# Splitting the next slot ahead of the norm, unread products between two tiles' transposes, and a first panel begun by parts

## The reference

```python
x = x + hybrid_mixer(rmsnorm(x, ...))              # gated delta rule and mLSTM
x = x + memory_cross_attention(rmsnorm(x, ...), rmsnorm(mem, ...), ...)
x = x + peer_ffn(rmsnorm(x, ...), ...)             # 128 key pairs, top 16, experts
x = rmsnorm(x, norm_final_w)
# second block: each sub-layer is followed by a layer norm
x = post_norm(x, swiglu(x, ...), g, b)             # layer_norm(DN_ALPHA * x + sub, g, b)
x = post_norm(x, chunked_sgu_mixer(x, ...), g, b)
x = post_norm(x, swiglu(x, ...), g, b)
# keys and values (selected, window, compressed) are made of this x
x = post_norm(x, swiglu(x, ...), g, b)
x = post_norm(x, sparse_attention(x, ...), g, b)
x = post_norm(x, swiglu(x, ...), g, b)
```

## Time and profile before

| | us or share |
|---|---|
| median of three runs | 2404.67 (2404.33 to 2405.97) |
| span of the profiled execution | 2405.3; no other time of that execution is given |
| TensorE busy | 2268.6, 94% |
| VectorE busy | 1544.9, 64% |
| ScalarE busy | 1126.1, 47% |
| mean granted TensorE clock | 0.964 |
| HBM over the span | 161 GB/s |

### The profile page before, as it was taken

The page is one execution under the profiler, slowest core; times in us unless marked ns, Lnnn a source line. Parts: engine busy times, 40 slices in busy tenths (PEclk is TensorE's granted clock), DMA queues, the critical chain, the costliest instruction groups (busy, mean ns, idle before and its releaser), DMA issues. The chain is left out here.

```text
span 2405.3 us, 38363 instructions
## 1 busy us (share of the span) xinstructions
PE 2268.6 (94%) x15466; PEld 2086.1 (87%) x15466; DVE 1544.9 (64%) x2713; ACT 1126.1 (47%) x1961; POOL 51.6 (2%) x26
## 2 busy tenths in 40 slices
PE   8979888999999999999999999999999999988998
PEld 8867676999999997888878998979998899867997
DVE  7866445999888985666655456665456545575554
ACT  5523334455554445555555344444443434474443
POOL 0121000100000000000000000000000000000000
PEclk9989889999999999999999999999999999889999
DMA  6362233355444445666646555535555655303552
GB/s 260 139 67 91 88 129 127 120 178 182 158 142 148 144 147 177 193 195 194 195 127 251 182 187 211 193 134 215 191 178 192 228 183 186 125 19 123 197 188 105
DMA packets 78310, 390.25 MB, mean 162 GB/s; under 512 B 9772, under 2 KB 12716, under 8 KB 49741
## 3 DMA queue, kind: packets, MB, share of 16 engines
q1 hardware_dynamic: 76684, 383.59, 46.3%
q0 software_dynamic: 1040, 4.19, 1.6%
q10 hardware_dynamic: 432, 0.33, 0.0%
HBM read 382.83 MB, written 5.24 MB: 161 GB/s over the span
## 5 line engine op out<-in xcount | busy, mean ns | idle before, releaser
L246 DVE TENSOR_TENSOR split_slots<-ring,split_slots 128x1024 fp32r<-128x1024 f32 x406 | 481.9, 1232 | 333.7 <-ACT split_slots L237 333.6
L339 PE MATMUL banks<-x_transposed_hi,split_slots 128*128 128x256 f32 x1920 | 549.8, 286 | 8.8 <-DVE split_slots L246 5.2
L340 PE MATMUL banks<-x_transposed_lo,split_slots 128*128 128x256 f32 x1920 | 547.9, 285 | 0.0
L341 PE MATMUL banks<-x_transposed_hi,split_slots 128*128 128x256 f32 x1920 | 547.6, 285 | 0.0
L237 ACT ACTIVATE split_slots<-ring 128x1024 fp32r<-128x1024 f32 x406 | 404.4, 1049 | 222.6 <-PE banks L341 197.2
L350 DVE SCALAR_TENSOR_TENSOR expert_lo<-ring,expert_hi 128x512 fp32r<-128x512 f32 x512 | 363.2, 714 | 173.8 <-ACT expert_hi L345 172.7
L345 ACT ACTIVATE expert_hi<-ring 128x512 fp32r<-128x512 f32 x512 | 323.2, 632 | 266.8 <-PE banks L341 266.7
L339 PEld LDWEIGHTS banks<-x_transposed_hi,split_slots 128*128 128x128 f32 x1920 | 372.2, 194 | 11.5 <-DVE split_slots L246 5.6
L340 PEld LDWEIGHTS banks<-x_transposed_lo,split_slots 128*128 128x128 f32 x1920 | 372.1, 194 | 1.5
L341 PEld LDWEIGHTS banks<-x_transposed_hi,split_slots 128*128 128x128 f32 x1920 | 372.1, 194 | 0.0
L339 PE MATMUL banks<-x_transposed_hi,expert_hi 128*128 128x256 f32 x1024 | 296.8, 290 | 5.5 <-DVE expert_lo L350 5.5
(11 more groups left out here) (463 smaller groups left out, 3431.8 us busy)
## 6 DMA issues: line engine op xcount, KB each, us to landing
ring<-in_ffn_w SPq DMA_DIRECT2D x132, 1024.0 KB, 4.8
ring<-in_peer_u SPq DMA_DIRECT2D x128, 512.0 KB, 3.5
ring<-in_peer_v SPq DMA_DIRECT2D x128, 512.0 KB, 4.3
ring<-in_w_in SPq DMA_DIRECT2D x16, 1024.0 KB, 5.1
ring<-in_sgu_w_in SPq DMA_DIRECT2D x16, 1024.0 KB, 4.8
ring<-in_peer_wq SPq DMA_DIRECT2D x8, 1024.0 KB, 5.0
ring<-in_sgu_w_out SPq DMA_DIRECT2D x8, 1024.0 KB, 4.8
ring<-in_kv_w SPq DMA_DIRECT2D x6, 1024.0 KB, 4.8
```

The lines of the kernel that those rows point to most:

```text
L246: ins = dve.tensor_tensor(self.parts[:, b, 1, p], self.k.w.slot(g)[:, p], self.parts[:, b, 0, p].bitcast(F32), ALU.subtract)
L339: pe.matmul(out, lh, rh, start=start, stop=False)
L340: pe.matmul(out, lh, rl, start=False, stop=False)
L341: return pe.matmul(out, ll, rh, start=False, stop=stop)
```

## The change

Three things, in the diff's order. Split buffers are numbered by the slot's number in the whole program instead of in its stage, so the next stage's first slot goes to the buffer of slot `slots - 3`; in PostNorm the begun slot's split always stands ahead of the norm, after a wait for that slot, and in RmsNorm it moves from last place to ahead of the norm (ScalarE) and ahead of the first add (VectorE). TensorE gets plain 128x128 float32 products of two constant tiles into bank 1, which nothing reads (`stand_in`): 3 after tile 0's transposes and, except in PostNorm 0, 7 when tile 1 is centred and 4 when its root is there; in RmsNorm 4, 6 and 4. Tile 1's transposes move out of the norm and into `high_first` of the next stage where there is one in the same block: with x on the right (weights stationary) the first four transposes, the 16 products of chunks 0 to 3, the other four transposes, the 16 products of chunks 4 to 7; with x on the left (`spatial_gating`) the 16 products of tile 0, then all eight transposes, then tile 1's products by halves. That first panel goes to bank 0 instead of 4. Where a barrier follows, `last` (or no `begin`) keeps the eight transposes in the norm.

```diff
@@ class Splitter
+    def buffer(self, n):
+        return (self.g0 + n) % self.buffers
...
-        g, b = self.g0 + n, n % self.buffers
+        g, b = self.g0 + n, self.buffer(n)
...
@@ class Beginning
+        self.b = self.g % BUFFERS
...
-        act.activation(k.split_parts[:, 0, 0, p], k.w.slot(self.g)[:, p], ACT.Copy).then_inc(self.high_done, 1)
+        act.activation(k.split_parts[:, self.b, 0, p], k.w.slot(self.g)[:, p], ACT.Copy).then_inc(self.high_done, 1)
...
@@ def high_first
-    before.rows_high(pe)
-    for j in range(2):
-        for c in range(DC):
+    started = []
+    def banks():
+        for signal, value in before.banks_read:
+            pe.wait_ge(signal, value)
+    def high(j, chunks):
+        for c in chunks:
             (lh, ll), (rh, rl) = operands(j, c)
-            pe.matmul(out(j), lh, rh, start=(j == 0 and c == 0), stop=False)
+            pe.matmul(out(j), lh, rh, start=not started, stop=False)
+            started.append(c)
             if x_on_right:
                 pe.matmul(out(j), ll, rh, start=False, stop=False)
             else:
                 pe.matmul(out(j), lh, rl, start=False, stop=False)
+    near, far = range(DC // 2), range(DC // 2, DC)
+    if before.turn is None:
+        banks()
+        if before.highed:
+            pe.wait_ge(*before.highed)
+        for j in range(2):
+            high(j, range(DC))
+    else:
+        if not x_on_right:
+            pe.wait_ge(before.highed[0], 2)
+            high(0, range(DC))
+        before.turn(pe, near)
+        if x_on_right:
+            banks()
+        else:
+            before.turn(pe, far)
+        pe.wait_ge(before.highed[0], 3)
+        for j in range(2) if x_on_right else (1,):
+            high(j, near)
+        if x_on_right:
+            before.turn(pe, far)
+        pe.wait_ge(before.highed[0], 4)
+        for j in range(2) if x_on_right else (1,):
+            high(j, far)
     before.rows_low(pe)
...
@@ def turn_chunks
-def turn_chunks(pe, k, src, tile, ready, first=0, normed=None):
-    for c in range(DC):
+def turn_chunks(pe, k, src, tile, ready, first=0, normed=None, own=range(8)):
+    for c in own:
         if normed is not None and c % 4 == 0:
             pe.wait_ge(normed, 2 * tile + c // 4 + 1)
         ins = pe.transpose(k.psum[:, first + 2 * tile + c // 4, c % 4 * P:(c % 4 + 1) * P], src[:, c * P:(c + 1) * P],
                            k.ident[:, :])
         if c % 4 == 3:
             ins.then_inc(ready, 1)
+def stand_in(pe, k, n):
+    for _ in range(n):
+        pe.matmul(k.psum[:, 1, 0:P], k.ident[:, :], k.ones[:, :], start=True, stop=True)
...
@@ class PostNorm
-        self.free = (slots - 1) // BUFFERS * BUFFERS
-        self.early = self.free < slots - 2
+        self.free = slots - BUFFERS
...
-        if self.begin and self.early:
+        if self.begin:
             self.begin.lows(dve)
...
-            if not self.early:
-                self.begin.lows(dve)
             for b in range(4):
                 self.low(dve, b)
...
-        if self.begin and self.early:
+        if self.begin:
             self.split.finished(act, self.free)
             self.begin.highs(act)
...
-            if not self.early:
-                act.wait_ge(self.tile_done, TILES)
-                self.begin.highs(act)
             self.high(act, 2)
             self.high(act, 3)
...
-        self.k.before = Before((self.tile_done, TILES), (self.highed, 4), (self.written, 4), ((self.written, 1),))
+        self.k.before = Before((self.tile_done, TILES), (self.highed, 4), (self.written, 4), ((self.written, 1),),
+                               turn=self.turn_last)
         self.k.gains_free = self.normed
+    def turn_last(self, pe, chunks):
+        turn_chunks(pe, self.k, self.k.x[:, 1, :], 1, self.banks, 4, self.normed, chunks)
     def tensor(self, pe):
         if self.begin:
-            for i in range(TILES):
-                turn_chunks(pe, self.k, self.k.x[:, i, :], i, self.banks, 4, self.normed)
+            turn_chunks(pe, self.k, self.k.x[:, 0, :], 0, self.banks, 4, self.normed)
+            stand_in(pe, self.k, 3)
+            if self.which != 0:
+                pe.wait_ge(self.negated, 2)
+                stand_in(pe, self.k, 7)
+                pe.wait_ge(self.rooted, 2)
+                stand_in(pe, self.k, 4)
+            if self.last:
+                self.turn_last(pe, range(DC))
...
@@ class RmsNorm
+        self.free = slots - BUFFERS
...
+        if self.begin:
+            self.begin.lows(dve)
         add(0)
         dve.wait_ge(*self.gain_landed)
...
-        if self.begin:
-            self.begin.lows(dve)
...
+        if self.begin:
+            self.split.finished(act, self.free)
+            self.begin.highs(act)
         act.activation(self.warm[:, :], k.eps[:, 0:1], ACT.Sqrt)
         squares(0)
...
-        if self.begin:
-            act.wait_ge(self.tile_done, TILES)
-            self.begin.highs(act)
+    def turn_last(self, pe, chunks):
+        turn_chunks(pe, self.k, self.xn[:, 1, :], 1, self.banks, 4, self.normed, chunks)
     def tensor(self, pe):
-        for i in range(TILES):
-            turn_chunks(pe, self.k, self.xn[:, i, :], i, self.banks, 4, self.normed)
+        turn_chunks(pe, self.k, self.xn[:, 0, :], 0, self.banks, 4, self.normed)
+        stand_in(pe, self.k, 4)
+        pe.wait_ge(self.added, 2)
+        stand_in(pe, self.k, 6)
+        pe.wait_ge(self.rooted, 2)
+        stand_in(pe, self.k, 4)
+        if not self.begin:
+            self.turn_last(pe, range(DC))
...
@@ def swiglu, def spatial_gating
-        norm = PostNorm(k, ctx, split, gains, which, 3 * UNITS, final)
+        norm = PostNorm(k, ctx, split, gains, which, 3 * UNITS, final, last=compress is not None)
-        norm = PostNorm(k, ctx, split, gains, 1, slots, squares=v[:, :, 0:D])
+        norm = PostNorm(k, ctx, split, gains, 1, slots, squares=v[:, :, 0:D], last=True)
-                    return k.psum[:, 4 + m % 2, j * SEQ:(j + 1) * SEQ]
+                    return k.psum[:, 4 + m % 2 if m else 0, j * SEQ:(j + 1) * SEQ]
-                act.activation(dst, bank2(k, 4 + m % 2), ACT.Gelu).then_inc(panel_read, 1)
+                act.activation(dst, bank2(k, 4 + m % 2 if m else 0), ACT.Gelu).then_inc(panel_read, 1)
```

More of the change, by code:

```diff
@@ L255, in panel @@
     def panel(self, n):
-        return [self.parts[:, n % self.buffers, q, :].rearrange("p (c n) -> p c n", c=DC) for q in range(2)]
+        return [self.parts[:, self.buffer(n), q, :].rearrange("p (c n) -> p c n", c=DC) for q in range(2)]
     def rows(self, n):
-        return [self.parts[:, n % self.buffers, q, :].rearrange("p (r n) -> p r n", r=2) for q in range(2)]
+        return [self.parts[:, self.buffer(n), q, :].rearrange("p (r n) -> p r n", r=2) for q in range(2)]
     def finished(self, engine, n, i=0, per=0):
@@ L289, in low @@
         dve.wait_ge(self.high_done, half + 1)
-        ins = dve.tensor_tensor(k.split_parts[:, 0, 1, p], k.w.slot(self.g)[:, p], k.split_parts[:, 0, 0, p].bitcast(F32),
-                                ALU.subtract)
+        ins = dve.tensor_tensor(k.split_parts[:, self.b, 1, p], k.w.slot(self.g)[:, p],
+                                k.split_parts[:, self.b, 0, p].bitcast(F32), ALU.subtract)
         if half == 1:
@@ L296, with __init__ @@
 class Before:
-    def __init__(self, splits_eaten, highed=None, written=None, banks_read=()):
+    def __init__(self, splits_eaten, highed=None, written=None, banks_read=(), turn=None):
         self.splits_eaten, self.highed, self.written, self.banks_read = splits_eaten, highed, written, banks_read
+        self.turn = turn
     def rows_high(self, pe):
@@ L2407, with __init__ @@
 class PostNorm:
-    def __init__(self, k, ctx, split, gains, which, slots, final=False, squares=None):
+    def __init__(self, k, ctx, split, gains, which, slots, final=False, squares=None, last=False):
+        self.last = last
         self.k, self.split, self.gains, self.which, self.slots = k, split, gains, which, slots
```

## The result

The changed kernel takes 2389.52 us (median of four runs: 2385.17, 2387.11, 2391.92, 2392.33) against 2404.50 for the kernel before beside it: a ratio of 0.9935, 95% interval 0.9923 to 0.9947. It was forecast at 2386.1, in a range of 2380 to 2397. The profiled execution took 2391.92, with a span of 2390.1, 15.2 us less than the 2405.3 of before.

What follows compares the result with a forecast made beforehand. TensorE, busy 94% of the span, was taken as the bound, losing time to idle and half clock at seven norms. Their gains sum to 18.6 us, from the median 2404.67 to 2386.1 us; range 2380 to 2397.

Steps and rivals of the forecast that it cites:

- N1: RmsNorm whose first transposes start at 324 us; next stage's panel 1 forecast to come 5.2 us sooner.
- N5: PostNorm 2, first transposes at 1809 us, x on the right; panel 1 forecast 1.7 us sooner.
- N7: PostNorm 4, first transposes at 2200 us; like N5 plus the early split, panel 1 forecast 2.8 us sooner.
- N3: PostNorm 0, first transposes at 1461 us; next panel's products run in the hole, panel 1 forecast 4.5 us sooner.
- A: Rival: the clock falls despite stand-ins, so only the order's 4.6 us remain, giving 2400 us; chance 0.13.
- B: Rival: next stage's splits come late at N1, N3, N5, N7 and loads lose time, about 2392 us; chance 0.12.
- C: Rival: stand-ins delay tile 1's transposes at six norms, not N3; 2412 us at 0.55 us each; chance 0.03.
- D: Rival: nothing measurable, the gain swallowed in PEER and attention, 2401 to 2407 us; chance 0.04.
- Then the order alone remains ... N3 2.6, N1 1.5, N7 0.8, N5 -0.3: Under A, gains in us from the new order at these norms with products at half rate; the rest 0, total 4.6.
- This path still has a 0.6 us hole for each copy: At N5, TensorE still idles 0.6 us for each transposed bank's copy, the second copy now behind 16 products.
- N4: PostNorm 1, first transposes at 1612 us, ending a stage; forecast gain 1.3 us, between ends 0 and 2.5.
- N6: PostNorm 3, first transposes at 2062 us, ending a stage; forecast gain 2.4 us, between ends 0.7 and 2.4.

Runs made afterwards that it cites:

- both turns together: Changed kernel with, where x is on the right, all eight transposes ahead of the first 16 products: 2384.24 us, ratio 0.9910; repeated, 2386.01 us, 0.9926.

## Why the prediction was right, and where it was not

**What held.** The forecast's mechanism is the one that the runs show. The idle between a norm's two tiles costs twice. Filled with stand-ins it no longer costs the clock: 1.00 through N1, N5 and N7, tile 1's transposes at 0.60 to 0.63 us per four. The hole itself stays (the transposes of tile 1 start 4.43 us after the first ones at N5, 4.32 before); only at N3, where products of the next panel run in it, does it cost neither. A stand-in costs 0.22 us, as taken from the earlier trace rows. That the split is hidden ahead of the norm at N1 and N7 held too, and the first products at N1 no longer wait for it. The Trainium skill, "TensorE: Matmul & The Clock Gate", section "HAM oscillation — how this bites in real kernels", warns only of longer gaps. The runs go against it: the level falls behind holes of 2.94 and 3.29 us in the kernel before and of 3.03 at N1 with this change's stand-ins taken out, and with them it stays. The prediction says that by the page the sum would keep A's 4.6; but those 4.6 are worked out with the clock falling, which by the page it would not, so the figure does not follow from it.

**Rivals.** The prediction's A, that the clock falls in spite of the stand-ins, is refuted by the clock of 1.00 and by 2389.52 where it had 2400. What it priced, the order with a falling clock, was then measured without stand-ins: 7.6 us where it had 4.6. B did not come: L376's only wait for a split of slots is the 5.2 us of before, at PEER. C is priced right: it is a matter of the number; 14 are under the limit, for tile 1's transposes start 4.07 us after the first ones at N1 and 4.42 at N5 with 14 as with none. D is out by its interval. The chance for faster, 0.88, is 0.865 when its parts are added up.

**"Then the order alone remains ... N3 2.6, N1 1.5, N7 0.8, N5 -0.3".** This step failed in its parts. Measured without stand-ins: N3 4.87, N1 2.40, N7 -0.08, N5 -0.97. It let the clock fall at N3 although the order puts 16 products into that very hole. So the forecast's 4.5 at N3 is right in size, and it owes nothing to the stand-ins there. At N5 and N7 it gave the queue of far transposes behind half-rate products too little; at N1 it came out 0.9 too low, and why there is open.

**"This path still has a 0.6 us hole for each copy".** Mis-sized: the holes are 0.78 and 0.69, together with the transposes 1.40 us before the first products (1805.75 - 1804.35) where the sum had 1.25. With this, a start 0.1 later than worked out, and 0.15 from the second round to the end of the low part, panel 1 is 13.03 us behind the first transposes at N5 and N7, not 12.6. That is 0.9 of the 1.7 us by which the sites' 16.9 fall short of 18.6. The prediction saw that the second copy stood behind 16 products, but did not ask for the order without that; it is worth 1.4 us at each of three sites. N3, on the other hand, came out 0.37 above its 4.5: VectorE went into slot 1's split without a pause and ended it 9.6 us after the first transposes, where the sum had 10.0.

**N4 and N6** were guesses between ends, and both came out 0.3 to 0.4 below. The level holds over the pause of 2.0 us at N6, and falls for a shorter time at N4. It is luck in part: with both turns together it held at both places in one profile of that kernel and fell at both in the other.

**"Everything after each place hangs on TensorE ... so I carry it to the end".** This holds behind N3: N4 to N7 and the end moved by the sites' own gains to within 0.1 us each. It fails behind N1, where 1.4 us were lost in memory attention to a new fall of the clock, behind a hole of 1.78 us that had cost nothing before. Why the same hole costs in one run and not in the other is not settled. The fall is there in both profiles of the change, with the early split alone, with the late split and with half of the stand-ins, and absent in the other seven profiles and in that of the kernel before.

**The early split** was put at the wait that it removes (3.3 us at N1, 0.8 at N7), and alone it is worth that: 3.07 and 0.61. Inside the changed kernel, taking it out costs 6.7 and 4.2 at these sites. The parts lean on each other: a late split opens a new hole behind the stand-ins.

**What is luck.** The forecast's 18.6 stands against 15.2 between the two profiles: 1.7 is missing at the sites, most of the rest in memory attention. The medians' 15.0 came out 3.6 short, and the second time the change was run, on another chip, it gained 13.6. The range had room for this by its allowance for the clock's falls elsewhere and for rival B; the sum itself had put them at nothing.

## What to carry to other kernels

Where a normalisation leaves TensorE idle for some 3 us between two tiles, put real products of the next panel there first, and unread ones where there are none; price them with the nearest row of the same shape, keep their sum under the hole, and see in the granted clock whether fewer do. Keep short transposes together ahead of the products that need only some of them, so that each copy runs beside products. Look at what a wait stands in front of in the engine's order before moving the work that it waits for.

## What the runs showed of the hardware

The full level survived holes that were far from full: at N5, with seven stand-ins, TensorE was busy 2.72 of 4.00 us and the clock read 1.00. At three stand-ins two norms with the same holes came out differently in one run (N5 1.00, N7 0.50). In the kernel before, the transposes behind the hole of 3.29 us ran at the full level at N4 (1.32 us for eight, the clock fell near 1618, in the pause after them), and at the lower one behind the same hole at N3 and N6 (1.97). A hole of 1.78 us in memory attention lowered the clock in the changed kernel and not in the kernel before. And behind the pause of 2.0 us at N6, one kernel read 1.00 in one execution (2052.7 us) and 0.50 in another (2054.3 us), with the same instructions right before it. So the length of a hole does not settle it, and neither do the instructions next to it: something that changes from execution to execution counts too. That it is where the hole lies in time fits all of this, but no run here tests it.
